# The odd layer's projection, latents and two attentions: narrow products packed, three stages made one

## The reference

```python
qc, kc, vc, qi, ki, wi, cq, ckv, kr = split_cols(x @ w_in, ODD_SIZES)   # 512,64,64,256,64,4,256,128,32
out_c = dsa_attention(qc, kc, vc, qi, ki, wi)
q = (rms_norm_2(cq, q_norm_g) @ w_uq).reshape(B, S, 8, 64 + 32)
kv = (rms_norm_2(ckv, kv_norm_g) @ w_ukv).reshape(B, S, 8, 64 + 64)
q = concat([q[..., :64], rope(q[..., 64:], pos)])
k = concat([kv[..., :64], broadcast(rope(kr, pos), 8 heads)])
out_d = causal_block_attention(q, k, kv[..., 64:])
return concat([out_c, out_d]) @ w_o
```

## Time and profile before

| | |
|---|---|
| Runs shown | 2096.48, 2099.99, 2104.41 us; median 2099.99 |
| Profiled execution | 2086.48 us, span 2084.8 us |
| Busy in the span | PE 94%, DVE 32%, ACT 19%, POOL 4% |
| Mean granted TensorE clock | 0.958 of 2.4 GHz |
| The four stages, `odd_in` to `odd_d` | 1429.0 to 1681.3 us of the span |

### The profile page before, as it was taken

One profiled execution on the slowest core, in us unless ns is written; L12 is line 12 of the kernel. 1 busy time (PEld: TensorE's weight loads), 2 busy tenths in 40 slices (PEclk: granted clock), 3 DMA queues, 4 the chain that ended last, 5 costly groups with the idle time before them and its releaser, 6 DMA issues.

```text
span 2084.8 us, 23327 instructions
## 1 busy us (share of the span) xinstructions
PE 1957.5 (94%) x9814; PEld 890.1 (43%) x9814; DVE 671.2 (32%) x1600; ACT 401.6 (19%) x869; POOL 82.2 (4%) x106
## 2 busy tenths in 40 slices
PE   7999999999999999999997999998998997999997
PEld 3464444444444445445553333335644444333322
DVE  3736322223300233106444000023776645200005
ACT  3203011111100013106501111112125511111111
POOL 0001000000000000000001100010000000200001
PEclk9989999999999999998996999999989997999999
DMA  4203822211221122201234999991110243799995
GB/s 153 68 21 101 333 80 81 81 68 44 80 71 61 61 94 81 81 1 41 102 136 153 348 397 397 394 387 58 41 41 1 81 162 135 232 398 395 398 381 202
DMA packets 140634, 335.57 MB, mean 161 GB/s; under 512 B 4536, under 2 KB 12744, under 8 KB 140400
## 3 DMA queue, kind: packets, MB, share of 16 engines
q1 hardware_dynamic: 126384, 283.80, 37.4%
q0 software_dynamic: 10976, 37.76, 4.7%
q10 hardware_dynamic: 3168, 12.50, 1.5%
HBM read 310.94 MB, written 23.09 MB: 160 GB/s over the span
## 4 chain that ended last, share of the span: by engine, by line
PE 86%; DMA 6%; DVE 4%; ACT 2%; issue 1%; DVEq 0%; SPq 0%; ACTq 0%
PE psum L601 39%; PE psum L1035 21%; PE psum L872 7%; DMA ring<-in_moe_w_up 5%; PE psum L805 5%; PE psum L947 3%; PE psum L976 2%; PE psum L960 2%; PE psum L1129 1%; PE psum L1016 1%; PE psum L747 1%; PE psum L613 1%; ACT ring L1485 1%; PE psum L1060 0%; PE psum L701 0%
## 5 line engine op out<-in xcount | busy, mean ns | idle before, releaser
L1035 PE MATMUL psum<-ring,scratch 128*32 128x512 f32 x3840 | 517.1, 603 | 13.5 <-DMA ring<-in_moe_w_up 10.6
L601 PE MATMUL psum<-xT,ring 128*128 128x512 f32 (+5 forms) x1152 | 465.2, 564 | 15.3 <-DVE xT L1708 4.5
L601 PEld LDWEIGHTS psum<-xT,ring 128*128 128x128 f32 (+2 forms) x1152 | 210.1, 190 | 266.0 <-issue 257.0
L1035 PEld LDWEIGHTS psum<-ring,scratch 128*32 128x32 f32 x3840 | 142.6, 111 | 300.3 <-issue 296.1
L601 PE MATMUL psum<-ring,xT 128*128 128x512 f32 (+4 forms) x704 | 240.7, 499 | 2.5 <-ACTq L1238 1.6
L601 PEld LDWEIGHTS psum<-ring,xT 128*128 128x128 f32 x704 | 121.3, 196 | 119.2 <-issue 111.0
L872 PE MATMUL psum<-ring,scratch 128*128 128x512 f32 x352 | 152.7, 593 | 1.8 <-PE psum L872 1.5
L1035 PE MATMUL psum<-xT,scratch 128*32 128x512 f32 x768 | 131.5, 612 | 6.5 <-DMA ring<-in_moe_w_up 6.5
L1649 DVE SCALAR_TENSOR_TENSOR scratch<-psum,overlay,scratch 128x511 f32<-128x511 f32 x88 | 65.9, 749 | 222.3 <-ACT scratch L1417 220.8
L2184 DVE TENSOR_TENSOR scratch<-psum,scratch 128x512 f32<-128x512 f32 x24 | 16.6, 692 | 336.1 <-PE psum L1035 336.1
L805 PE MATMUL psum<-xT,ring 128*128 128x512 f32 x224 | 101.5, 609 | 2.4 <-DVEq L1638 2.3
(11 more groups left out here) (374 smaller groups left out, 1657.8 us busy)
## 6 DMA issues: line engine op xcount, KB each, us to landing
ring<-in_moe_w_gate SPq DMA_DIRECT2D x28, 2048.0 KB, 14.8
ring<-in_moe_w_up SPq DMA_DIRECT2D x28, 2048.0 KB, 18.0
ring<-in_moe_w_down SPq DMA_DIRECT2D x24, 2048.0 KB, 13.8
ring<-in_w_up SPq DMA_DIRECT2D x11, 2048.0 KB, 9.3
xT<-in_moe_w_down SPq DMA_DIRECT2D x8, 2048.0 KB, 10.9
expert_rows<-scratch ACTq DMA_DIRECT2D x20, 512.0 KB, 7.5
ring<-in_w_down SPq DMA_DIRECT2D x4, 2048.0 KB, 8.3
ring<-in_even_w_in SPq DMA_DIRECT2D x4, 2048.0 KB, 8.4
```

The costliest lines, as they stand in the source:

```text
L601: mm = nc.tensor.matmul(out_, lhsT, rhs, start=(j == 0), stop=(j == len(pairs) - 1))
L1035: mm = nc.tensor.matmul(bank[r, :], lhsT[:, t, r], w_[:, t, c0:c0 + 512], start=(t == 0), stop=(t == nk - 1))
```

## The change

The columns of the odd projection are loaded in another order, the first chunk in four pieces ((896, 992), (1348, 1380), (640, 896), (512, 640)). One `features` product now makes index keys, index weights and kr together, and one makes kC and vC; 4 transposes of 4 rows and 4 of 64 rows turn the index weights and vC to token order. Index products take 64 rows each, the two heads of a pair on different row halves; ACT writes the index keys to both halves, and nothing is zeroed. kr is rotated with one 32 x 32 matmul, by POOL (three passes of 32 x 512), and copied to the 8 heads by ACT.

The latents are normalised, transposed and multiplied in `odd_in`: DVE does so after four of the 16 rounds for n = 3 (`pick(NT - 1, 4)`), and picks on. ACT, not DVE, empties the transposed latents. `abreast` makes narrow products side by side on column tiles: the rotary query parts four heads at a time (32 columns each, all 128 partitions of a bank), the plain query parts and the keys two heads at a time (64 columns each). The rotation takes 2 matmuls of 128 x 128, not 8 of 96 x 96; DVE multiplies two banks by the sine, two tiles by the cosine, and adds in 8 passes of 32 x 512. Stage `latent` is gone, and `odd_c` and `odd_d` are one stage `odd_cd` of 32 pairs. Index queries, relu buffers, `ckvT` and rotary parts lie in ring slot 0.

The diff, in this order: loads, stages, PE, ACT, DVE, POOL and SP; `evicted(k)` waits until bank k's product is emptied.

```diff
-    plan += [("odd_w_in_2", 0, 8, a, b - a) for a, b in ((512, 964), (964, 1380), (0, 512))]
+    plan += [("odd_w_in_2", 0, 8, ((896, 992), (1348, 1380), (640, 896), (512, 640)), 512)]
+    plan += [("odd_w_in_2", 0, 8, a, b - a) for a, b in ((964, 1348), (0, 512))]
...
-    "odd_in", "odd_c", "latent", "odd_d", "odd_out", "route1", "experts1", "overflow1", "combine1",
+    "odd_in", "odd_cd", "odd_out", "route1", "experts1", "overflow1", "combine1",
...
-        enter_features("combine0", f, [(w_, 384, HD), (w_, P, P)])
+        enter_features("combine0", f, [(w_, 0, P), (w_, P, P)])
         features(f, ODD_IN, 2, a0, c0, 2 * P)
+        evicted(0)
         for n in range(NT):
-            tokens(f, ODD_IN, 3 + n, a0, c0, n, 448, 452)
+            mm = nc.tensor.transpose(banks[K_WEIGHTS][:, 4 * n:4 * n + 4], wIT[HD:HD + 4, n * P:(n + 1) * P],
+                                     ident[HD:HD + 4, HD:HD + 4])
...
+        for k, (n, h) in enumerate(INDEX, K_INDEX):
+            r = slice(h % 2 * HD, (h % 2 + 1) * HD)
             bank_emptied(f, ODD_IN, k)
+            nc.tensor.matmul(banks[k % 8][:, 0:(n + 1) * P], qI[r, h // 2, n * P:(n + 1) * P],
+                             kI[r, 0:(n + 1) * P], start=True, stop=True).then_inc(f.mm, 1)
+        features(f, ODD_IN, K_KEY, a0, c0, 3 * P)
...
+        def abreast(k, w_, first, width, d0, rhs):
+            bank_emptied(f, ODD_IN, k)
+            for t, to in enumerate(rhs):
+                for i in range(P // width):
+                    mm = nc.tensor.matmul(banks[k % 8][i * width:(i + 1) * width, :], w_[:, t, first + i, d0:d0 + width], to,
+                                          start=(t == 0), stop=(t == len(rhs) - 1))
+            mm.then_inc(f.mm, 1)
...
+        evicted(K_TURN_C + 1)
+        for g in range(2):
+            abreast(K_ROT + g, uq, 4 * g, ROT, HD, [cqT[:, t, :] for t in range(2)])
+        for j in range(4):
+            abreast(K_NOPE + j, uq, 2 * j, HD, 0, [cqT[:, t, :] for t in range(2)])
...
+        for g in range(2):
+            evicted(K_ROT + g)
+            bank_emptied(f, ODD_IN, K_TURN_Q + g)
+            nc.tensor.matmul(banks[(K_TURN_Q + g) % 8][:, :], operand["turn"], rotary[:, g, :], start=True, stop=True)\
...
+        for j in range(4):
+            abreast(K_KEY_D + j, ukv, 2 * j, HD, 0, [ckvT])
+        for n in range(NT):
...
+        def rotary_keys():
+            act.wait_ge(keys_rotated, 1)
+            A(kD[HD:MLA, :, :], krT[P - ROT:P, :].unsqueeze(1).to_broadcast([ROT, 8, T]), ACT.Copy)
+
+        evacuate(f, ODD_IN, jobs, {K_LATENT + NT - 1: squared, K_QUERY: rooted, K_QUERY + 2: rotary_keys})
...
+        pick(NT - 1, 4)
         dve.wait_ge(odd_sq, NT + 1)
         step(V.reciprocal(rstd, rstd))
...
+        pick(NT - 1, TOPK // 8 - 4)
+        picked(NT - 1)
+        for g in range(2):
+            dve.wait_ge(f.mm, K_TURN_Q + g + 1)
+            V.tensor_tensor(rotary_sin[:, g, :], banks[(K_TURN_Q + g) % 8][:, :], operand["sin"], ALU.mult).then_inc(f.v, 1)
+            step(V.tensor_tensor(rotary[:, g, :], rotary[:, g, :], operand["cos"], ALU.mult))
+            for i in range(4):
+                r = slice(i * ROT, (i + 1) * ROT)
+                V.tensor_tensor(qD[HD:MLA, 4 * g + i, :], rotary[r, g, :], rotary_sin[r, g, :], ALU.add)
+        for n in range(NT):
+            dve.wait_ge(f.mm, K_VALUE_D + n + 1)
+            V.tensor_copy(vD[:, n, :], banks[(K_VALUE_D + n) % 8][:, :]).then_inc(f.v, 1)
...
-        clear_halves(kI)
+        pool.wait_ge(F["odd_in"].a, odd_count(K_TURN_KR))
+        step(G.tensor_tensor(krT[r, :], krT[r, :], operand["cos"][r, :], ALU.mult))
+        step(G.tensor_tensor(kr_turned[r, :], kr_turned[r, :], operand["sin"][r, :], ALU.mult))
+        G.tensor_tensor(krT[r, :], krT[r, :], kr_turned[r, :], ALU.add).then_inc(keys_rotated, 1)
...
+        for q, src in pieces(c):
+            sp.dma_start(slot_view(at, c)[:, :, q], src).then_inc(w_loaded[slot_of[at]], 16)
```

301 lines of the change are left out of this document (125 added, 176 removed).

## The result

The changed kernel takes **2040.68 us** (median of 4 runs, 2040.08 to 2042.54); the kernel before, in 4 runs beside it, 2098.23 us (2094.99 to 2104.41). The ratio is 0.9724, 95% interval 0.9699 to 0.9748: 57.5 us less, where 54 were forecast, and inside the range of 2037 to 2067.

A forecast was written before the change was run, and what follows sets the result against it. The projection was taken as bound by two nearly equal paths, PE's products and DVE's choice of keys. Terms 9.5 + 41.3 + 4.1 - 1 = 53.9, say 54 us, off 2100 gave 2046 us; range 2037 to 2067.

The forecast's parts named there:

- What bounds it: Projection: PE's products and DVE's choice of keys nearly equal paths; shortening PE's alone gets no more than about 5 us.
- Start of the index: Projection: four transposes (0.5 us) replace 64 instructions (10.01 us), DVE's sum takes 7.7; DVE picks 11.5 us earlier.
- The bounded price: Latents' narrow products: a pair of 64 columns taken at 0.22 us, between ends of 0.22 and 0.44.
- DVE's last stretch: End of projection: rotation 7.5 us, four value copies 2.5; C starts at 1540.6, 9.5 us less.
- The rule against it: Skill's rule that tiling does not speed PSUM emptying; if PE alone set end, C at about 1538, sum 56 or 57.
- Latent gone: The old latent stage, from 1595.26 to 1636.53, disappears: 41.3 us less.
- C and D in one: Seam between C and D: emptying and filling the pipeline, 6.7 us, is mostly saved: 4.1 us less.
- Loads: First weight chunk in four pieces shares DMA engines with the experts' gathers: 1 us more, between 0 and 8.
- The signs that I named: Trace signs: odd_out at about 1627 instead of 1681.3; core wrong if stages in front of the projection end later than 1429.
- the rival that it stays up at C's start: Rival: clock does not drop to 0.50 at C's start; 4 us taken, no more than 5.6; 2042 us; chance 0.12.
- tiles that don't run side by side: Rival: narrow products take 0.44 us each, C starts at 1561, 20 us worse, 2066 us; chance 0.08.
- the half clock through the attention: Rival: clock stays at 0.50 through C and D, 66.6 us more, 2113 us; chance 0.02.

The follow-up runs named there:

- first profile of after: The changed kernel's first profiled execution: 2042.54 us; first odd_in product to first odd_out product 196.55 us, beside 252.31 in the kernel before.
- the second profile: The changed kernel profiled again without edits: execution 2030.94 us; first odd_in product to first odd_out product 194.78 us.
- same_tile: Changed kernel with all narrow latent products on one column tile, one after another; first odd_in to first odd_out product 214.72 us, beside 196.55.
- weights_by_tokens: Changed kernel with index weights made by 64 products again, without the 4 transposes; first odd_in to first odd_out product 209.39 us, beside 196.55.
- pick_first: Changed kernel with all 16 pick rounds for the last query tile before the latents' norms; first odd_in to first odd_out product 210.12 us, beside 196.55.
- shared_end: Changed kernel with one of four rotary additions on POOL, three of four value copies on ACT; first odd_in to first odd_out product 196.15 us.
- two_stages: Changed kernel with C and D as two stages again; C's last transposes to D's first 6.72 us; first odd_in to first odd_out product 198.78 us.
- contiguous: Changed kernel with the first weight chunk loaded as one contiguous block, not four pieces; first odd_in to first odd_out product 197.01 us, beside 196.55.
- the first pair: First profiles of the kernel before and the changed one: 2086.48 and 2042.54 us; first odd_in to first odd_out product 252.31 and 196.55 us.

## Why the prediction was right, point by point

The forecast was made against the first landmark at 1429.0, so I compare times from there (forecast; measured in the first profile of after).

| step | forecast | measured |
|---|---|---|
| index products start | +25.3 | +24.3 |
| DVE starts to pick | +34.3 | +32.7 |
| mask ready | +101.4 | +99.8 |
| rotation starts | +101.4, PE due at +100 to +103 | +100.4, PE last by 0.6 |
| rotation (8 additions, 4 passes) | 7.5 us | 8.2 us |
| value copies | 2.5 us | 2.5 us |
| C starts | +111.6, 9.5 earlier | +111.2, 9.9 earlier (9.1 in the second profile; 9.4 on equal terms of the clock) |
| latent gone | 41.3 us | 41.3 us |
| seam | 4.1 us | 3.8 us |
| C itself | 0 | 0.8 us less (3.4 in the second) |
| loads | 1 us more | 0 |

- *What bounds it* held. PE's products and DVE's choice of keys end within 0.6 us of each other, at the rotation. same_tile lengthened PE's path alone, by 20.5 us, and cost 19.0 at C's start; weights_by_tokens held up both paths (11.5), and pick_first made PE wait for DVE and DVE then for PE (13.4). So little on PE's side was hidden any more. That DVE's choice of keys is as long a path rests on the trace; no run shortened it alone.
- *Start of the index*: transposes 0.41 us for 0.5, and DVE's sum 7.25 us for 7.7. The picks start 13.1 us earlier, not 11.5. Of the 1.6 us, 1.0 is the start of the index products, and 0.8 of that is luck: the products ahead of them end at +23.5 where the 64 began at +24.3, because less of the half clock at the landmark lay behind it. In the second profile they end at +24.3 and the picks start 12.3 us earlier. The transposes took 0.1 less, and the sum gave 0.45. The index products themselves took 4.14 us at full clock, for which I had 5 to 8.
- *The bounded price*, a pair of 64 columns, was 0.22 us by the near end. In the keys, 3.65 / 16 = 0.23. The 64 products of the queries took 10.66 for 10.5.
- *DVE's last stretch*: four additions take 2.78 us, 0.70 each; I had taken the shorter of the two pitches in the earlier trace rows, 0.61. 0.7 us too little in all. *ACT* and *POOL* cost nothing, as forecast; POOL's three small passes were 1.3 us each.
- *The rule against it*: PE had all products of the projection done at 1545.08 and DVE at 1547.75, so C waited 2.83 us for DVE's end. The Trainium skill (TensorEngine Tiling (Array Packing), PSUM Bottleneck) says that tiling speeds up TensorE but not the emptying of PSUM, which may then become the bottleneck. The trace agrees in part: DVE is last, but of its 10.7 us behind the rotation only the two sine passes and the four copies, 3.9 us, empty PSUM; the other 6.8 are passes in SBUF. If PE alone had set the end, C would have come at about +108.4; DVE's rows gave the better number. shared_end, which shared this work out, gained 0.4 us.
- *Latent gone* and *C and D in one* are what they were said to be. Two stages in a row give a seam of 6.72 us (two_stages), the 6.7 that stood in before beside latent; one stage gives 2.92, where I had allowed 2.6.
- *Loads* cost nothing (contiguous): the +1 was wrong, on the safe side.
- *The signs that I named*: the two numbers of `odd_out`, 1627 forecast and 1633.2 measured, differ because the stages in front ended at 1436.68 instead of 1429. I had named that as a sign of a wrong core; it wasn't one: those 7.7 us lie in the experts' products, and the same products took 284.7 to 286.7 us on one chip and 291.8 to 294.2 on another.
- *The clock*: the rival that it stays up at C's start was priced at 4 us, by 16 us at half clock. It came in part: 13.7 us low in one profile, 6.8 in the other, worth 0.8 and 3.4 us against before. The sum had nothing for it, and this is most of what came on top of the forecast. With PE kept busy the clock did stay up, and C took 35.50 us, 5.9 less than before. So the price of 4 was too low, and the bound of 5.6, which let ACT's busy time set the end, was 0.3 too low. It isn't one case or the other but varies from one execution to the next.
- *The other rivals* fell: tiles that don't run side by side would have brought C to +130.2 (same_tile; I had +132), and the half clock through the attention never showed.

The sum of the steps, 55.8 us in the first pair and 57.5 in the second, and the medians, 57.5 and 58.8, agree. Against the forecast of 54 the step that was mis-sized is the clock in C (0 for 0.8 and 3.4), with 1 us for the loads that weren't there; the start of C, latent and the seam, 54.9 in the sum, came to 54.5 on equal terms of the clock. Of the 5 us between the forecast time of 2046 and the measured 2040.68, 3.5 are that gain and 1.8 the kernel before, whose median beside it was 2098.23 and not 2100. The 13.5 us between the first profile of before and its median, which the prediction left open, lie outside the odd layer as far as the traces go: the kernel before took 2086.21 and 2089.02 us on chip 12, 2099.97 on chip 5 and 2090 to 2105 on chip 14, and two experts' stages, each some 7 us longer on chip 5 than on chip 12 in the changed kernel's variants, make about that (an estimate: no profile of before was taken on chip 5 or 14). Why the same products take longer there stays open.

## What to carry to other kernels

Where two queues feed the same point, put both side by side and ask which is last there after the change: here 20.5 us added on PE's side cost 19.0 at C's start, because the change had already used up the slack. Measure a changed stretch between two landmarks of the trace, since the whole span of one execution moved by 10 us and more with the code untouched, and compare the granted clock at both landmarks too. And where a narrow product costs as much as a wide one, either transpose what has been computed already or lay the narrow ones on different column tiles; both paid here.

## What the runs showed of the hardware

- **Half clock behind a short pause varies.** After 2.8 us without work for PE, C went to 0.50 within 1.3 to 2.2 us of its start in two executions of one program and stayed there for 13.7 or 6.8 us, which moves C by 2.6 us. Over all thirteen profiles C's length goes by the time at half clock in it, from 35.50 us with none to 41.88 with 17.1. Three products in the pause kept it at 1.00; one, with 1.57 us left idle, did not, and in same_tile, with 0.89 us idle and no filler, it fell too, for 10.2 us. So the pause as the cause is supported, not settled, and whether the three products pay in the median is open: that kernel has one time only.
- **Column tiles** of 64 columns share the array as fully as those of 32: on one tile an instruction of 512 columns takes 0.43 to 0.44 us in either width; in pairs of 64 it takes 0.22 to 0.23, and in fours of 32 0.11 (3.57 us for 32). The order of the tiles in the stream is free (10.74 us and 10.66).
- **POOL can hold up DVE** on small passes: a DVE addition of 32x512 that starts together with one of POOL's (1.26 us) took 1.80 us, against 0.68 without POOL. DVE's MAX8 and MATCH_REPLACE8 passes did not suffer: 0.56 and 0.54 us beside POOL's three passes of the rotary key, as elsewhere. POOL's passes took 1.26 to 1.27 in both places.
- **Products of 4 columns** take 0.15 us each and run at a clock of 0.72, and the next ones, at 0.63, pay for it too (6.52 us for 4.14 in the changed kernel, where four transposes stand in front of them).
- **One program, two chips.** The same 2304 instructions of the experts (tiles 128*32 of L1042) kept PE busy for 257 to 259 us in the profiles on chip 12 and for 263 to 265 on chip 5, in the first of the two stages. Each chip had one batch of runs, so that chip and time can't be told apart.
